# Swapping the halves of a rotary embedding by small DMAs inside SBUF instead of by a matrix product

## The chip, the core and the metric

The kernel runs on one core of one Trainium2 chip. The metric is device time in microseconds (us) for one execution, the median of several; lower is better. Engines: PE is TensorE (matrix products), DVE is VectorE, ACT is ScalarE, POOL is GpSimd, SP is SyncE, which here only issues DMAs, in the order of its program, and waits for semaphores between them.

## The reference

The reference is one hybrid layer followed by two layers of a second kind, over 512 tokens of width 1024. In each layer of the second kind the normalised input is multiplied by a wide weight matrix whose columns are queries, keys and values of several attention mixers, and some of these get a rotary embedding:

```python
def hybrid_mixer(x, w_in, ...):
    h = split_columns(x @ w_in)
    y_a = mla_mixer(h['mla_cq'], h['mla_ckv'], h['mla_krope'], ...)      # rotates krope and 32 of 96 columns of each query head
    y_b = nsa_mixer(h['nsa_q'], h['nsa_k_cmp'], ...)                     # rotates its queries and keys
    y_c = dsa_mixer(h['dsa_q'], h['dsa_k'], ..., h['idx_q'], h['idx_k'], ...)   # rotates all of these
    y_d = stick_breaking_mixer(h['sb_q'], h['sb_k'], h['sb_v'])
    ...
```

The rotation of a head of width n takes its first half a and its second half b to (a cos - b sin, b cos + a sin), with an angle for each token and pair. So it needs, beside the value itself, the value of the other half.

## The kernel before

Activations lie with features on the 128 partitions and 512 tokens along the row. All weights come through one stream of slabs, each 128 x 1024 in float32 (eight 128x128 tiles, 512 KB), loaded by SP into a ring of `RAW = 3` buffers (`load_slabs`, L519 to L531). Most slabs are then split for products in three parts: ACT makes a rounded copy `w_hi` (`high_slabs`, L545), POOL or DVE makes the rest `w_lo` (`low_slabs`, L560); these two have a ring of `SPLIT = 3` buffers. A raw buffer of a split slab is free when its `w_lo` is made; that of a slab used unsplit is free when the last product that reads it is done. ACT takes its part of the splitting in program order: before it moves the result of job j out of PSUM it splits all slabs up to two behind that job's own, and for each it waits until the slab has landed.

The stage that the change touches is `gemm_phase` as `Layer.run` calls it, once for each of the two layers of the second kind. Its jobs are, in order:

- 14 jobs of 24 products (8 tiles, three products each; one slab each): kvcmp, dki, iq0, iq1, cq0, cq1, ckv, kk, nq0, nq1, dq0, dq1, sq0, sq1. Four unsplit slabs, used by short products of the helper `Compress` (L2560), lie in the stream between the slabs of iq1 and cq0, cq0 and cq1, cq1 and ckv, ckv and kk
- 4 jobs mq0 to mq3 (the query heads of the first mixer; two float32 tiles each, all on one unsplit slab)
- 4 jobs uk0 to uk3 and 2 jobs uv0, uv1 on the next unsplit slab, which `Compress` also reads for its last products (L2568, L2570). They are followed in the stream by the slabs of sk0 and sk1, the first that the stage behind uses

Work of other helpers is put between the jobs by `Features`: index scores of one mixer (PE L2694, ACT L2703, DVE L2718 and L2715), sums of squares (ACT L865, PE L836), and splits of finished keys and queries (ACT L2744, L2762, DVE L2749, L2767, POOL L2758). The stage uses three PSUM banks for the jobs in turn: job j's product waits until job j-3's result is moved out (`taken`). At its end all engines meet (L392) before the next stage, an attention, begins.

Thirteen jobs have a rotary embedding: kvcmp, dki, iq0, iq1, kk, nq0, nq1, dq0, dq1, mq0 to mq3. For each, in this order:

1. ACT moves the sum out of PSUM to its tile of `big` (L693) and signals `taken`.
2. PE multiplies that tile by a 128x128 matrix of 0, 1 and -1, in float32, into PSUM bank 4 or 5 (L651). In PE's program this product stands behind the whole next job.
3. DVE multiplies the product by the sine table into a scratch tile (L714), the tile by the cosine table (L716), and adds the two (L718), which signals `joined`.

DVE does step 3 of job j-1 in its step j, ahead of the helpers' work of that step, and so on in program order. SP's part of the stage is the loading of slabs alone.

Of the kernel before, what the change touches and what calls it, by code (L numbers as in the profile page):

```python
# [21 lines left out]
P = 128  # L22
T = 512
QB = T // P
D = 1024
KD = D // P
# [36 lines left out]
SLAB = 8  # L63
# [172 lines left out]
for _n in ("h2", "i4", "mq", "kx"):  # L236
    ROPE.add("cos_" + _n, T)
    ROPE.add("sin_" + _n, T)
for _n in ("h2", "i4", "mq", "kx"):
    ROPE.add("rot_" + _n, P)  # L240

VEC1 = Columns()
for _n, _w in (("norm1_g", 8), ("norm2_g", 8), ("b_mq", 4), ("b_mk", 4), ("b_mo", 4), ("b_fq", 4), ("b_fk", 4),
# [12 lines left out]
def constants():  # L256

    c = np.zeros((P, CONST.n), np.float32)
    rope = np.zeros((P, ROPE.n), np.float32)

    def put(name, a):
        where, to = (ROPE, rope) if name in ROPE.at else (CONST, c)
        at, n = where.at[name]
        to[: a.shape[0], at:at + n] = a

    put("ident", np.eye(P))
    put("ones", np.ones((P, P)))
    put("negident", -np.eye(4))
    put("negroot", -np.eye(4) * np.sqrt(128.0))

    def rotation(spans):

        r = np.zeros((P, P))
        for a, n in spans:
            for i in range(n // 2):
                r[a + n // 2 + i, a + i] = -1
                r[a + i, a + n // 2 + i] = 1
        return r

    def tables(spans):  # L280
        cos, sin = np.ones((P, T)), np.zeros((P, T))
        for a, n in spans:
            inv = np.float32(10000.0) ** (-np.arange(0, n, 2, dtype=np.float32) / np.float32(n))
            ang = (np.arange(T, dtype=np.float32)[None, :] * inv.astype(np.float32)[:, None]).astype(np.float32)
            for half in range(2):
                cos[a + half * n // 2:a + (half + 1) * n // 2] = np.cos(ang.astype(np.float64))
                sin[a + half * n // 2:a + (half + 1) * n // 2] = np.sin(ang.astype(np.float64))
        return cos, sin

    for kind, spans in (("h2", [(0, 64), (64, 64)]), ("i4", [(32 * i, 32) for i in range(4)]),  # L290
                        ("mq", [(64, 32)]), ("kx", [(0, 64), (64, 32), (96, 32)])):
        put("rot_" + kind, rotation(spans))
        cos, sin = tables(spans)
        put("cos_" + kind, cos)
        put("sin_" + kind, sin)
    i = np.arange(P)

    before = np.zeros((P, T - P))
    put("causal", np.concatenate([before, np.where(i[None, :] <= i[:, None], 0, NEG)], 1))
    put("strict", np.where(i[None, :] < i[:, None], 0, NEG))  # L300
    put("tri", (i[:, None] <= i[None, :]).astype(float))
    put("chunk_tri", ((i[:, None] <= i[None, :]) & (i[:, None] // CHUNK == i[None, :] // CHUNK)).astype(float))
    ends = np.arange(NCMP) * CMP_STRIDE + CMP_LEN - 1
    seen = ends[None, None, :] <= (np.arange(QB)[None, :, None] * P + i[:, None, None])
    floor = np.full((P, QB, 1), NEG / 10)
    put("cmp_neg", np.concatenate([np.where(seen, 0, NEG), floor], 2).reshape(P, -1))
    put("goes_on", np.tile((np.arange(T) % CHUNK != 0).astype(float), (P, 1)))
    put("rms_eps", np.full((P, 1), RMS_EPS))
    put("ln_eps", np.full((P, 1), LN_EPS))
    put("one", np.ones((P, 1)))  # L310
    return c, rope
# [16 lines left out]
class Core:  # L328
# [189 lines left out]
            self.last_sum[at // SLAB + slab] = self.sums  # L518
        return [self.sums - jobs + 1 + b for b in range(jobs)]  # L519

    def load_slabs(self, sp):

        last = max(self.last_sum) if self.last_sum else -1
        while self.loaded < min(NSLABS, last + 1 + RAW):
            n = self.loaded
            if n >= RAW and n - RAW in SPLIT_AT:
                sp.wait_ge(self.lo_made, SPLIT_AT[n - RAW] + 1)
            elif n >= RAW:
                sp.wait_ge(self.sums_done, self.last_sum[n - RAW])
            sp.dma_start(self.raw[:, n % RAW, :], self.weights[n]).then_inc(self.slab_loaded[n % RAW], 16)  # L530
            self.loaded += 1  # L531
# [88 lines left out]
def gemm_phase(k, jobs, norm=None, scalar=None, vector=None, banks=None, bank=0, between=None, after=None, lows=True):  # L620
# [7 lines left out]
    for j, job in enumerate(jobs):  # L628
        ends += k.use([tiles_of(job)], by_slab=False)
        if between:  # L630
            between.use(j)
    taken, rotated, joined, part = [k.flag(n) for n in ("taken", "rotated", "joined", "rope_part")]
    ropes = [j for j, job in enumerate(jobs) if job.get("rope")]
    banks = banks or (4 if ropes or norm else 8)

    with k.block() as block:
        @block.sync
        def _(sp):
            k.load_slabs(sp)

        @block.tensor
        def _(pe):
            if norm:
                norm.tensor(pe)

            def rotate(r):
                job = jobs[ropes[r]]
                pe.wait_ge(taken, k.at(taken, ropes[r] + 1))
                if r >= 2:
                    pe.wait_ge(k.flag("rope_part"), k.at(k.flag("rope_part"), 2 * r - 3))  # L650
                nc.tensor.matmul(k.ps[:, 4 + r % 2, :], k.rope("rot_" + job["rope"]), job["out"],  # L651
                                 start=True, stop=True).then_inc(rotated, 1)

            if between:
                between.tensor(pe, -1)
            for j, job in enumerate(jobs):
                if j >= banks:
                    pe.wait_ge(taken, k.at(taken, j - banks + 1))
                for signal in after.get(j, ()) if after else ():
                    pe.wait_ge(*signal)  # L660
                for c, (part, i, cols, start, stop) in enumerate(job["sum"]):
                    if i is not None:
                        k.need(pe, i)
                    if "wait_tile" in job:
                        job["wait_tile"](pe, c)
                    for m, (lhsT, rhs) in enumerate(part):
                        mm = nc.tensor.matmul(k.ps[:, bank + j % banks, cols], lhsT, rhs, start=(start and m == 0),  # L667
                                              stop=(stop and m == len(part) - 1))
                mm.then_inc(k.sums_done, 1)
                if j - 1 in ropes:  # L670
                    rotate(ropes.index(j - 1))
                if between:
                    between.tensor(pe, j)
            if len(jobs) - 1 in ropes:
                rotate(len(ropes) - 1)

        @block.scalar
        def _(act):
# [20 lines left out]
        if ropes or norm or vector or between:  # L699
            @block.vector  # L700
            def _(dve):
# [6 lines left out]
                for j in range(len(jobs) + 1):  # L708
                    if j - 1 in ropes:
                        r, job = ropes.index(j - 1), jobs[j - 1]  # L710
                        rows = slice(0, job.get("rope_rows", P))
                        turned, to = k.scr[rows, 10 + r % 2, :], job["out"][rows]
                        dve.wait_ge(rotated, k.at(rotated, r + 1))
                        nc.vector.tensor_tensor(turned, k.ps[rows, 4 + r % 2, :], k.rope("sin_" + job["rope"])[rows],  # L714
                                                ALU.mult).then_inc(part, 1)
                        nc.vector.tensor_tensor(to, to, k.rope("cos_" + job["rope"])[rows], ALU.mult).then_inc(part, 1)  # L716
                        dve.wait_ge(part, k.at(part, 2 * r + 2))
                        nc.vector.tensor_tensor(to, to, turned, ALU.add).then_inc(joined, 1)  # L718
                    if between and j < len(jobs):
                        between.vector(dve, j)  # L720
# [9 lines left out]
        norm.passed()  # L730
    if between:
        between.passed()
    k.passed(taken=len(jobs), rotated=len(ropes), joined=len(ropes), rope_part=2 * len(ropes))


def token_phase(k, x, jobs, norm, loads=(), bias_here=None, first=0, taken="taken"):
# [2274 lines left out]
def copy_in_phase(k, x, first, later, norm):  # L3011

    nc, s = k.nc, norm.s
    norm.lands = False
    tile_here = [k.flag(f"x_here{c}") for c in range(KD)]
    first_here, here = k.flag("norm_here"), k.flag("inputs_here")
    with k.block() as block:
        @block.sync
# [34 lines left out]
        def _(pe):  # L3053
            pe.wait_ge(first_here, k.at(first_here, 16 * len(first)))
            pe.wait_ge(tile_here[0], 16)
            for _ in range(5):
# [3 lines left out]
            pe.wait_ge(s["squared"], norm.at("squared", KD))  # L3060
            nc.tensor.matmul(k.ps[:, 5, :], k.c("ones"), norm.square_at(KD - 1), start=False, stop=True)\
                .then_inc(s["sq_summed"], 1)
    return here, 16 * len(later)


# [147 lines left out]
def layer_start(k, l, norm):  # L3213
# [3 lines left out]
    ln1 = ResidNorm(k, "ln1_g", "ln1_b")  # L3217
    glu_phase(k, *w["ffn1"], norm, ln1)
    token_phase(k, lambda c: (k.in_hi[:, c, :], k.in_lo[:, c, :]), [(w["v"], lambda tb: big[:, tb, :], None)], ln1,
                loads=[(big[:, 33:42, :].rearrange("p a b -> p (a b)"), k.rope_dram)], first=QB, taken="laid")  # L3220


class Layer:
# [15 lines left out]
    def run(self):  # L3239
# [10 lines left out]
        for key, i in at.items():  # L3250
            scale = 64 ** -0.5 if key in ("nq0", "nq1", "dq0", "dq1", "sq0", "sq1") else 1.0
            jobs.append(feature_job(k, x, w[key], tile(i), rope=rope.get(key), scale=scale,
                                    rope_rows=64 if key == "kvcmp" else P))
        names = list(at)
        for h in range(HEADS):
            jobs.append(feature_job(k, lambda c: tile(6 + c), w["uq"][h], tile(25 + h), depth=2, split=False, rope="mq",
                                    scale=96 ** -0.5))
        for h in range(HEADS):
            jobs.append(feature_job(k, lambda c: tile(8), w["uk"][h], tile(29 + h)[0:64], depth=1, split=False,
                                    view=lambda at: at[0:64]))  # L3260
# [184 lines left out]
```

## Time and profile before

| | |
|---|---|
| median of 3 runs | 3339.65 us (3339.61 to 3339.69) |
| the profiled execution's own time | 3335.59 us |
| its span, first to last instruction | 3333.8 us |
| PE busy | 3231.3 us, 97% of the span |
| DVE, ACT, POOL busy | 1483.1, 1272.9, 383.7 us |
| slab loads | 503, of 512 KB |
| the stage with the rotary embeddings | about 1474 to 1594 us, and 2598 to 2717 us |

PE is busy nearly throughout, so its time is close to the kernel's. The duration that the profile gives a product is longer than the distance at which the next follows, since products are pipelined; distances between starts tell what one costs.

### The profile page before, as it was taken

The page shows a single profiled execution, that of the slowest core. Times are in us where ns is not written, and L with a number is a line of the kernel's source. Part 1 is how long each engine was busy: PE and PEld are TensorE (multiplying, and loading weights), DVE is VectorE, ACT ScalarE, POOL GpSimd, SP SyncE. Part 2 cuts the span into 40 slices and gives each one's busy share as a digit, 9 for nine tenths or more (in the row PEclk, how much of TensorE's full clock was granted, in tenths as well). Part 3 has the DMA queues.
Part 4 walks back from the last instruction along what each step waited for, and adds up shares of the span by engine and source line. Part 5 has one row for each costly group of instructions (what it writes and reads, how often), then busy time and mean ns, then how long its engine had stood idle before and what let it go on. Part 6 is the DMA issues. An engine that isn't in the chain of part 4 may idle for free. (4 is left out here: it accounts for less than half of the span.)

```text
span 3333.8 us, 37221 instructions
## 1 busy us (share of the span) xinstructions
PE 3231.3 (97%) x14860; PEld 2558.4 (77%) x14860; DVE 1483.1 (44%) x2260; ACT 1272.9 (38%) x2190; POOL 383.7 (12%) x277
## 2 busy tenths in 40 slices
PE   9999999999999999999979999999999998899998
PEld 7767778878888888877656888878887766578886
DVE  4154532244243333455875433343334478563333
ACT  3344642333132323235654432242222456542222
POOL 0412434400000000003410000000000233000000
PEclk9999999999999999999989999999999999999999
DMA  4211313323333333332001333323332310123332
GB/s 155 89 45 39 101 58 103 99 82 102 95 95 101 95 98 99 95 98 89 26 1 64 93 97 95 95 88 95 97 94 88 130 45 1 32 83 95 101 92 73
DMA packets 76060, 276.91 MB, mean 83 GB/s; under 512 B 8688, under 2 KB 8944, under 8 KB 75632
## 3 DMA queue, kind: packets, MB, share of 16 engines
q1 hardware_dynamic: 75888, 274.54, 26.7%
q8 instruction: 118, 1.93, 0.2%
q14 instruction: 54, 0.44, 0.0%
HBM read 272.41 MB, written 2.10 MB: 82 GB/s over the span
## 5 line engine op out<-in xcount | busy, mean ns | idle before, releaser
L545 ACT ACTIVATE w_hi<-raw_slabs 128x1024 fp32r<-128x1024 f32 x489 | 516.6, 1057 | 1235.5 <-PE ps L585 1128.8
L560 DVE TENSOR_TENSOR w_lo<-raw_slabs,w_hi 128x1024 fp32r<-128x1024 f32 x372 | 455.1, 1224 | 717.1 <-ACT w_hi L545 717.1
L585 PE MATMUL ps<-in_hi,w_hi 128*128 128x512 f32 x1840 | 719.1, 391 | 5.1 <-DVE in_lo L911 5.1
L585 PE MATMUL ps<-in_lo,w_hi 128*128 128x512 f32 x1840 | 715.9, 389 | 0.0
L585 PE MATMUL ps<-in_hi,w_lo 128*128 128x512 f32 x1840 | 715.8, 389 | 0.0
L585 PE MATMUL ps<-parts,w_hi 128*128 128x512 f32 x2240 | 693.5, 391 | 0.9 <-DVE scratch L1528 0.8
L560 POOL TENSOR_TENSOR w_lo<-raw_slabs,w_hi 128x1024 fp32r<-128x1024 f32 x117 | 288.0, 2463 | 2304.6 <-ACT w_hi L545 2287.6
L585 PEld LDWEIGHTS ps<-parts,w_hi 128*128 128x128 f32 x2240 | 420.4, 188 | 92.7 <-issue 4.3
L585 PE MATMUL ps<-parts,w_lo 128*128 128x512 f32 x1120 | 435.8, 389 | 0.0
L585 PEld LDWEIGHTS ps<-in_hi,w_hi 128*128 128x128 f32 x1840 | 345.4, 188 | 83.2 <-DVE in_lo L911 9.2
L585 PEld LDWEIGHTS ps<-in_hi,w_lo 128*128 128x128 f32 x1840 | 345.4, 188 | 72.1
L585 PEld LDWEIGHTS ps<-in_lo,w_hi 128*128 128x128 f32 x1840 | 345.5, 188 | 71.7 <-issue 1.0
L585 PEld LDWEIGHTS ps<-parts,w_lo 128*128 128x128 f32 x1120 | 210.2, 188 | 43.6
L667 PE MATMUL ps<-in_hi,w_hi 128*128 128x512 f32 x584 | 236.7, 405 | 1.2 <-POOL w_lo L560 1.2
L667 PE MATMUL ps<-in_hi,w_lo 128*128 128x512 f32 x584 | 227.6, 390 | 0.0
L667 PE MATMUL ps<-in_lo,w_hi 128*128 128x512 f32 x584 | 227.6, 390 | 0.0
L1314 DVE SCALAR_TENSOR_TENSOR big<-ps,scratch 128x512 f32<-128x512 f32 x88 | 60.6, 691 | 267.5 <-PE ps L585 248.3
L667 PEld LDWEIGHTS ps<-in_hi,w_hi 128*128 128x128 f32 x584 | 109.7, 188 | 31.6 <-issue 6.5
L667 PEld LDWEIGHTS ps<-in_lo,w_hi 128*128 128x128 f32 x584 | 109.7, 188 | 25.6 <-issue 3.8
L667 PEld LDWEIGHTS ps<-in_hi,w_lo 128*128 128x128 f32 x584 | 109.6, 188 | 23.3
L2063 ACT ACTIVATE scratch<-ps,stats 128x384 f32<-128x384 f32 (+4 forms) x176 | 85.4, 485 | 89.6 <-DVE stats L2034 70.8
L1890 PE MATMUL ps<-const_cols,scratch 128*128 128x128 f32 (+1 forms) x472 | 92.0, 291 | 18.2 <-ACT scratch L1938 15.9
(304 smaller groups left out, 3549.9 us busy)
## 6 DMA issues: line engine op xcount, KB each, us to landing
raw_slabs<-weights SPq DMA_DIRECT2D x503, 512.0 KB, 3.6
big<-rope SPq DMA_DIRECT2D x2, 2304.0 KB, 8.6
x_resid<-xT SPq DMA_DIRECT2D x8, 256.0 KB, 4.6
outT<-x_resid SPq DMA_DIRECT2D x8, 256.0 KB, 2.0
const_cols<-consts SPq DMA_DIRECT2D x1, 836.0 KB, 9.5
scratch<-brow SPq DMA_DIRECT2D x1, 768.0 KB, 10.1
vector_cols<-vec SPq DMA_DIRECT2D x2, 45.5 KB, 9.7
vector_cols<-vec SPq DMA_DIRECT2D x1, 68.5 KB, 3.5
```

The lines of the kernel that those rows point to most:

```text
L545: self.nc.scalar.activation(self.w_hi[:, m % SPLIT, :], self.raw[:, n % RAW, :], ACT.Copy)\
L560: (self.nc.gpsimd if i is None else self.nc.vector).tensor_tensor(self.w_lo[:, m % SPLIT, :], self.raw[:, n % RAW, :], self.w_hi[:, m % SP ...
L585: mm = k.nc.tensor.matmul(out, lhsT, rhs, start=(c == 0 and m == 0), stop=(last and m == 2))
L667: mm = nc.tensor.matmul(k.ps[:, bank + j % banks, cols], lhsT, rhs, start=(start and m == 0), stop=(stop and m == len(part) - 1))
L1314: nc.vector.scalar_tensor_tensor(made(f), k.ps[:, 2 * (f % 3) + 1, :], 0.5, k.scr[:, f % 2, :], ALU.mult, ALU.mult).then_inc(hidden, 1)
L1890: mm = k.nc.tensor.transpose(k.ps[0:w, bank, a:a + P], p[:, a:a + w], k.c("ident"))
L2063: nc.scalar.activation(probs(i)[:, 0:u.width], k.ps[:, bank(i), 0:u.width], ACT.Exp, bias=col(0, i), scale=u.scale, accum_out=col(1, i)).t ...
```

## The change

The rotation matrices are gone (the table that is loaded for each layer shrinks from 9 to 8 tiles of 128x512). In their place SP copies the halves: for each rotated span of n rows one DMA takes its upper n/2 rows of `big` to the lower place of a scratch tile, and one the reverse. That is 2 DMAs for kvcmp and for each of mq0 to mq3, 6 for dki, 8 for iq0 and for iq1, 4 for each of kk, nq0, nq1, dq0 and dq1: 52 in a layer, of 16 or 32 rows of 2 KB each. SP waits for the sum to be moved out (`taken`) and, from the third rotary job on, for the join of the rotary job two before (`joined`), whose scratch tile it fills anew. DVE then multiplies the scratch tile in place by a sine table that carries the sign, and goes on as before.

SP's program therefore alternates: ahead of the copies of each rotary job it issues those slab loads whose buffers can be free by then (up to five slabs past the job's own), and all others behind its copies. The rest of the loads come after the copies of mq3.

```diff
-    def load_slabs(self, sp):
+    def load_slabs(self, sp, upto=NSLABS):
         last = max(self.last_sum) if self.last_sum else -1
-        while self.loaded < min(NSLABS, last + 1 + RAW):
+        while self.loaded < min(NSLABS, last + 1 + RAW, upto + 1):
...
+    moves, landed = [], [0, 0]
+    for r, j in enumerate(ropes):
+        moves.append([(to, to + half, n // 2) for a, n in ROPE_SPANS[jobs[j]["rope"]] if a < jobs[j]["rope_rows"].stop
+                      for to, half in ((a, n // 2), (a + n // 2, -(n // 2)))])
+        landed[r % 2] += 16 * len(moves[r])
+        jobs[j]["swaps"] = landed[r % 2]
...
         @block.sync
         def _(sp):
+            for r, j in enumerate(ropes):
+                slab = max(tiles_of(jobs[j])) // SLAB
+                most = slab + (RAW if slab in SPLIT_AT else RAW - 1)
+                while most < slab + RAW + 2 and (most + 1 - RAW in SPLIT_AT or most + 1 - RAW <= slab - 1):
+                    most += 1
+                k.load_slabs(sp, most)
+                sp.wait_ge(taken, k.at(taken, j + 1))
+                if r >= 2:
+                    sp.wait_ge(joined, k.at(joined, r - 1))
+                for to, src, n in moves[r]:
+                    sp.dma_start(k.scr[to:to + n, 10 + r % 2, :], jobs[j]["out"][src:src + n]).then_inc(swapped[r % 2], 16)
             k.load_slabs(sp)
...
-            def rotate(r):
-                job = jobs[ropes[r]]
-                pe.wait_ge(taken, k.at(taken, ropes[r] + 1))
-                if r >= 2:
-                    pe.wait_ge(k.flag("rope_part"), k.at(k.flag("rope_part"), 2 * r - 3))
-                nc.tensor.matmul(k.ps[:, 4 + r % 2, :], k.rope("rot_" + job["rope"]), job["out"],
-                                 start=True, stop=True).then_inc(rotated, 1)
-
...
-                if j - 1 in ropes:
-                    rotate(ropes.index(j - 1))
...
-                        dve.wait_ge(rotated, k.at(rotated, r + 1))
-                        nc.vector.tensor_tensor(turned, k.ps[rows, 4 + r % 2, :], k.rope("sin_" + job["rope"])[rows],
+                        dve.wait_ge(swapped[r % 2], k.at(swapped[r % 2], job["swaps"]))
+                        nc.vector.tensor_tensor(turned, turned, k.rope("sin_" + job["rope"])[rows],
                                                 ALU.mult).then_inc(part, 1)
```

The mq jobs' cosine, sine and add now act on their 32 rotated rows only, instead of on 128. Semaphores of the first phase are reused for the copies.

## Rows read from the trace of the kernel before

**Rows 1.** The page: busy time of each engine, its share of the span.
```profile
PE 3231.3 (97%) x14860; PEld 2558.4 (77%) x14860; DVE 1483.1 (44%) x2260; ACT 1272.9 (38%) x2190; POOL 383.7 (12%) x277
```

**Rows 2.** Line L651, the rotation product: duration (ns), first and last start.
```profile
L651 PE MATMUL ps<-big x52: 590/591/667, 1484.7 to 2711.3; 128*128 128x512 f32 x52
```

**Rows 3.** Timeline of PE around a rotation product (one row left out): start, us, engine, line.
```profile
1484.49 0.39 PE L667 MATMUL ps<-in_hi,w_lo 128*128 128x512 f32 x1
1484.72 1.02 PE L651 MATMUL ps<-big 128*128 128x512 f32 x2
...
1485.82 0.40 PE L667 MATMUL ps<-in_lo,w_hi 128*128 128x512 f32 x1
```

**Rows 4.** Timeline between iq1's and cq1's products: ACT, PE, SP, POOL.
```profile
1497.61 0.60 ACT L693 ACTIVATE big<-ps 128x512 f32<-128x512 f32 x1 [4.80 <-PE ps L667]
...
1500.17 0.80 SPq L530 DMA_DIRECT2D raw_slabs<-weights  x2
...
1504.97 2.36 POOL L560 TENSOR_TENSOR w_lo<-raw_slabs,w_hi 128x1024 fp32r<-128x1024 f32 x1 [9.29 <-ACT w_hi L545]
...
1508.09 0.48 PE L667 MATMUL ps<-in_hi,w_hi 128*128 128x512 f32 x1
```

**Rows 5.** Timeline of ACT, and one PE row, around dq0 and dq1.
```profile
1551.11 0.60 ACT L693 ACTIVATE big<-ps 128x512 f32<-128x512 f32 x1 [3.16 <-PE ps L667]
...
1557.90 0.58 ACT L693 ACTIVATE big<-ps 128x512 f32<-128x512 f32 x1
...
1559.45 0.44 PE L2694 MATMUL ps<-parts 128*128 128x384 f32 x1 [0.23 <-ACT scratch L2703]
```

**Rows 6.** Timeline of the stage's end, DVE and POOL.
```profile
1574.10 3.32 DVE L2718 SCALAR_TENSOR_TENSOR big<-scratch,big 128x512 f32<-128x512 f32 x4 [1.79 <-ACT scratch L2703]
...
1583.09 0.68 DVE L714 TENSOR_TENSOR scratch<-ps,big 128x512 f32<-128x512 f32 x1
...
1586.44 0.68 DVE L714 TENSOR_TENSOR scratch<-ps,big 128x512 f32<-128x512 f32 x1
...
1591.60 0.69 DVE L718 TENSOR_TENSOR big<-big,scratch 128x512 f32<-128x512 f32 x1
...
1581.35 4.61 POOL L2758 TENSOR_TENSOR parts<-big,parts 64x512 fp32r<-64x512 f32 x3
```

**Rows 7.** Timeline of the stage's end: SP, ACT, PE.
```profile
1583.94 0.33 SPq L530 DMA_DIRECT2D raw_slabs<-weights  x1
...
1587.44 1.06 ACT L545 ACTIVATE w_hi<-raw_slabs 128x1024 fp32r<-128x1024 f32 x1 [2.89 <-DMA raw_slabs<-weights]
1588.40 0.57 ACT L693 ACTIVATE big<-ps 64x512 f32<-64x512 f32 x1
...
1588.19 2.74 PE L667 MATMUL ps<-big,raw_slabs 128*128 128x512 f32 x6
...
1594.42 0.38 PE L1882 MATMUL ps<-big 128*128 128x32 f32 x2 [1.15 <-PEq L392]
```

**Rows 8.** SP's DMAs: a line's issue (ns); from the page, us to landing.
```profile
L3021 SPq DMA_DIRECT2D x_resid<-xT x8: 384/432/433, 0.7 to 5.0; - x8
...
raw_slabs<-weights SPq DMA_DIRECT2D x503, 512.0 KB, 3.6
...
outT<-x_resid SPq DMA_DIRECT2D x8, 256.0 KB, 2.0
```

**Rows 9.** Lines L714 and L718, DVE: duration min/median/max (ns).
```profile
L714 DVE TENSOR_TENSOR scratch<-ps,big x26: 676/692/693, 1485.8 to 2713.9; 128x512 f32<-128x512 f32 x24, 64x512 f32<-64x512 f32 x2
...
L718 DVE TENSOR_TENSOR big<-big,scratch x26: 683/692/2772, 1487.1 to 2715.2; 128x512 f32<-128x512 f32 x24, 64x512 f32<-64x512 f32 x2
```

**Rows 10.** Windows behind the stage's end; the column after POOL's is PE's granted clock.
```profile
1593.30:1597.30 4.00, 2.21 (x13) 1.98 (x14) 2.15 (x10) 1.92 (x11) 2.35 (x1) 0.93 0.47 135
1597.30:1600.70 3.40, 3.40 (x13) 2.58 (x12) 1.94 (x10) 2.61 (x7) 1.07 (x3) 0.58 0.53 154
...
2720.30:2727.10 6.80, 6.71 (x20) 4.67 (x20) 4.52 (x17) 4.03 (x14) 2.77 (x7) 0.54 0.21 77
```

More of the change, by code:

```diff
@@ L238 @@
     ROPE.add("sin_" + _n, T)
-for _n in ("h2", "i4", "mq", "kx"):
-    ROPE.add("rot_" + _n, P)
+ROPE_SPANS = {"h2": ((0, 64), (64, 64)), "i4": tuple((32 * i, 32) for i in range(4)), "mq": ((64, 32),),
+              "kx": ((0, 64), (64, 32), (96, 32))}
 VEC1 = Columns()
@@ L269, in constants @@
     put("negroot", -np.eye(4) * np.sqrt(128.0))
[L271 to L278, printed above, removed]
     def tables(spans):
@@ L286, in tables @@
                 cos[a + half * n // 2:a + (half + 1) * n // 2] = np.cos(ang.astype(np.float64))
-                sin[a + half * n // 2:a + (half + 1) * n // 2] = np.sin(ang.astype(np.float64))
+                sin[a + half * n // 2:a + (half + 1) * n // 2] = (2 * half - 1) * np.sin(ang.astype(np.float64))
         return cos, sin
-    for kind, spans in (("h2", [(0, 64), (64, 64)]), ("i4", [(32 * i, 32) for i in range(4)]),
-                        ("mq", [(64, 32)]), ("kx", [(0, 64), (64, 32), (96, 32)])):
-        put("rot_" + kind, rotation(spans))
+    for kind, spans in ROPE_SPANS.items():
         cos, sin = tables(spans)
@@ L631, in gemm_phase @@
             between.use(j)
-    taken, rotated, joined, part = [k.flag(n) for n in ("taken", "rotated", "joined", "rope_part")]
+    taken, joined, part = [k.flag(n) for n in ("taken", "joined", "rope_part")]
+    swapped = [k.flag(f"tile_here{n}") for n in range(2)]
     ropes = [j for j, job in enumerate(jobs) if job.get("rope")]
+    moves, landed = [], [0, 0]
[4 more added lines that the diff above has]
+        jobs[j]["swaps"] = landed[r % 2]
     banks = banks or (4 if ropes or norm else 8)
@@ L669, in _ @@
                 mm.then_inc(k.sums_done, 1)
-                if j - 1 in ropes:
-                    rotate(ropes.index(j - 1))
                 if between:
                     between.tensor(pe, j)
-            if len(jobs) - 1 in ropes:
-                rotate(len(ropes) - 1)
         @block.scalar
@@ L710, in _ @@
                         r, job = ropes.index(j - 1), jobs[j - 1]
-                        rows = slice(0, job.get("rope_rows", P))
+                        rows = job["rope_rows"]
                         turned, to = k.scr[rows, 10 + r % 2, :], job["out"][rows]
-                        dve.wait_ge(rotated, k.at(rotated, r + 1))
-                        nc.vector.tensor_tensor(turned, k.ps[rows, 4 + r % 2, :], k.rope("sin_" + job["rope"])[rows],
+                        dve.wait_ge(swapped[r % 2], k.at(swapped[r % 2], job["swaps"]))
+                        nc.vector.tensor_tensor(turned, turned, k.rope("sin_" + job["rope"])[rows],
                                                 ALU.mult).then_inc(part, 1)
@@ L732, in gemm_phase @@
         between.passed()
-    k.passed(taken=len(jobs), rotated=len(ropes), joined=len(ropes), rope_part=2 * len(ropes))
+    k.passed(taken=len(jobs), joined=len(ropes), rope_part=2 * len(ropes), tile_here0=landed[0], tile_here1=landed[1])
 def token_phase(k, x, jobs, norm, loads=(), bias_here=None, first=0, taken="taken"):
@@ L3014, in copy_in_phase @@
     norm.lands = False
-    tile_here = [k.flag(f"x_here{c}") for c in range(KD)]
+    tile_here = [k.flag(f"tile_here{c}") for c in range(KD)]
     first_here, here = k.flag("norm_here"), k.flag("inputs_here")
@@ L3062, in _ @@
                 .then_inc(s["sq_summed"], 1)
+    k.passed(**{f"tile_here{c}": 16 for c in range(KD)})
     return here, 16 * len(later)
@@ L3219, in layer_start @@
     token_phase(k, lambda c: (k.in_hi[:, c, :], k.in_lo[:, c, :]), [(w["v"], lambda tb: big[:, tb, :], None)], ln1,
-                loads=[(big[:, 33:42, :].rearrange("p a b -> p (a b)"), k.rope_dram)], first=QB, taken="laid")
+                loads=[(big[:, 33:41, :].rearrange("p a b -> p (a b)"), k.rope_dram)], first=QB, taken="laid")
 class Layer:
@@ L3252, in run @@
             jobs.append(feature_job(k, x, w[key], tile(i), rope=rope.get(key), scale=scale,
-                                    rope_rows=64 if key == "kvcmp" else P))
+                                    rope_rows=slice(0, 64 if key == "kvcmp" else P)))
         names = list(at)
@@ L3256, in run @@
             jobs.append(feature_job(k, lambda c: tile(6 + c), w["uq"][h], tile(25 + h), depth=2, split=False, rope="mq",
-                                    scale=96 ** -0.5))
+                                    rope_rows=slice(64, 96), scale=96 ** -0.5))
         for h in range(HEADS):
```

## The prediction

> **What bounds the kernel now.** I read the page first: PE is busy 97% of the span [rows 1], so what counts is PE's time and what keeps PE waiting; on another engine an operation is free until PE or the meeting at the stage's end waits for it. Then the line of the rotation product, 52 instructions, two for each of 26 products [rows 2]. Then PE's timeline around one [rows 3]: ordinary products start 0.23 us apart (1484.49, 1484.72). The rotation starts at 1484.72, and the next job's second product at 1485.82; one product (0.23) lies between, so the rotation costs 1.10 - 0.23 = 0.87 us. Its two durations of 0.59 overlap and aren't its price. Last I read the timelines where PE could be made to wait once it runs ahead: the slab behind iq1 [rows 4], ACT around dq1 [rows 5], and the stage's end [rows 6, 7]. The second layer repeats the first there.
>
> **Removed.** 26 x 0.87 = 22.6 us of PE time, if PE could start its next work at once each time, and a wait of PE's for L714 of 1.4 us a layer before mq3's rotation. The four rotations of mq0 to mq3 (3.5 of 11.3 us a layer) lie in the tail, costed below; nine lie ahead of it (7.8 us). What remains of the nine, for one layer:
>
> *Four ahead of cq1* (kvcmp, dki, iq0, iq1: 3.5 us). cq1's slab goes into the buffer of the unsplit slab that PE reads right behind iq1's products. Before, its load left at 1500.17, its `w_lo` was made at 1504.97 + 2.36 = 1507.33, and PE came at 1508.09 [rows 4]: 7.16 us from issue to split, and PE 0.76 later. Now this load stands behind iq1's eight copies. ACT had moved iq1 out at 1497.61 + 0.60 = 1498.21; two rotations earlier (the third stands behind iq1's products) that is 1496.5, and dki's join, which the copies also wait for, is long done. From rows of other DMAs an issue takes 0.33 [rows 7] to 0.43 us [rows 8], so eight take 2.6 to 3.5, and the load leaves at 1499.1 to 1500.0. The slab is split 7.16 later, at 1506.3 to 1507.2, while PE would be there at 1508.09 - 3.48 = 1504.6. So 0.9 to 1.8 us are kept of 3.5; I take 1.3.
>
> *kk and nq0* (1.7): what follows kk's rotation are sums of squares that ACT makes at the same time, so some of it is waited away; I keep 1.3 (0.9 to 1.7).
>
> *nq1 and dq0* (1.7): the last index product behind dq1 waits for ACT (L2694 at 1559.45, idle before it, released by L2703), and ACT comes late to dq1 (1557.90), in one chain of its own work since 1551.11 [rows 5]. From dq0's end (about 1551) on ACT sets the pace; I keep 0.8 (0.4 to 1.7).
>
> *dq1* (0.9): the same shape, ACT's move and its first L2703 before the last index product; I keep 0.4 (0 to 0.9).
>
> Sum ahead of the tail: 1.3 + 1.3 + 0.8 + 0.4 = 3.8 us a layer, between 2.2 and 6.1.
>
> **The tail.** Here I count in the clock of before and subtract the 3.8 at the end. DVE does the index sums behind sq1 from 1574.10 without a break until 1583.09, then the four mq ropes until 1591.60 + 0.69 = 1592.29 [rows 6]. This chain hangs on sq1's products, not on the mq rotations; removing these doesn't shorten it. Step by step:
>
> 1. DVE's first multiply reads PSUM now and will read SBUF with both inputs, as L718 does. L714 never took more than 693 ns, L718 up to 2772 [rows 9]; the long ones lie beside POOL's work. In mq0's rope POOL runs L2758 until 1585.96 [rows 6], and the rope takes 3.35 us (1583.09 to 1586.44) where the other three take 5.85 / 3 = 1.95. With all three operations behind POOL I add one 0.65: mq0 joined at 1587.1, mq1 at 1589.0.
> 2. SP may copy mq3's halves only when mq1 is joined, 1589.0. Two issues and the semaphore: 1589.8 (to 1590.0).
> 3. Only then does SP issue the load of sk1's slab, which before left at 1583.94, as soon as mq3's products had used up its buffer [rows 7]. It lands 3.6 us later [rows 8], at 1593.4.
> 4. ACT is in program order. It waited for this slab before: L545 at 1587.44 was idle 2.89 us for the DMA, and uk0 was moved out only behind it, at 1588.40 [rows 7]. Now L545 starts at 1593.45, and uk0 is out at 1593.45 + 0.96 + 0.6 = 1595.0.
> 5. uk3 needs uk0's bank. Before, uk1, uk2, uk3 started from 1588.19 (six instructions, 0.86 a pair [rows 7]), so uk3 at 1589.9, and the next stage's first product at 1594.42, 4.5 later. Now uk3 starts at 1595.0 and the next stage at 1599.5: **+5.1 us** (4.5 to 5.6). DVE's last rope, with mq3's copies landing between 2.0 us [rows 8] and twice the slab's 3.6 after 1589.8, is done by 1599.0, so a slow copy stays just hidden.
>
> In this tail mq3's products end two rotations sooner, at 1583.9 - 1.7 = 1582.2, and uk0 to uk2 take 2.6 more; PE then has nothing from 1584.8 until 1595.0, some 10 us. Before, a stretch in which PE was busy 2.21 of 4.00 us was followed by 3.4 us at half clock in the first layer, and a like one by 6.8 us in the second (granted clock 0.58 and 0.54 in my windows, which cut the edges) [rows 10], so 1.2 GHz instead of 2.4. After 10 idle us I expect the same for the products from uk3 on. 3.4 to 6.8 us at half clock cost 1.7 to 3.4 us: **+2.5**.
> "TensorE: Matmul & The Clock Gate", section "HAM oscillation — how this bites in real kernels", of the Trainium skill says that PE idling over a DMA wait brings the clock down to half and that the work behind it starts cold. By that rule the 2.5 stands; without it the sum below would be 5.0 us less.
>
> On step 1 the Trainium skill, "SBUF — State Buffer", section "Who interferes with whom", says that a DVE instruction with two SBUF inputs contends with a GpSimd one that reads SBUF, while one with a single SBUF input doesn't. The trace agrees (693 against 2772 ns). Without it step 1 would be 0.65 less, the whole 1.3.
>
> Moved and added elsewhere: other copies are issued while SP would wait for a `w_lo` or a landing anyway, and the ropes of kvcmp to dq1 get their input after 2 to 4 us instead of after a whole job of 5.5, so DVE isn't later; if a copy took 8 us they would be. The smaller table load (8 tiles for 9) is hidden. L716 and L718 stay as they are.
>
> **Sum.** For a layer 5.1 + 2.5 - 3.8 = +3.8 us, for both +7.6. The profiled execution took 3335.59, so 3343.2; the median of the runs, 3339.65, lies 4.06 above that execution, so **3347 us**. Own range: each layer from 4.5 + 1.7 - 6.1 = +0.1 to 5.6 + 3.4 - 2.2 = +6.8, so 3340 to 3353, and up to 3356 if the next stage also runs longer at half clock.
>
> **Rivals.**
> - *PE's clock costs nothing net* (0.29). Half-clock stretches come already right behind the stage's end [rows 10]; if the one in the tail only takes their place, 2.5 drops out: 2 x (5.1 - 3.8) = +2.6, 3342. With most of the nine rotations kept (6.1) it is 3338. Within 0.2%.
> - *The slab isn't late* (0.13), the other side. All hangs on step 3: if DVE joined mq1 before about 1584, SP's load would leave as before, the tail would cost nothing, and the layers gain 3.8 each: 3332; with all 11.3 + 1.4 kept, 3314. For it: the earlier ropes get their input sooner and DVE has idle time ahead of 1574.10 (1.79 us). Against: DVE's work from there to mq0's rope waits for sq1's products, not for ropes.
> - *Copies land slowly* (0.08). If 16-row copies take 8 us or more, the helpers behind each rope on DVE wait, and the last rope ends past 1599: some 2 us a layer at the end and as much before, 3356.
>
> **Chances.** A measurement of this kernel tells about 0.2%, 6.7 us, from no change. Forecast 0.50, the rivals 0.29, 0.13 and 0.08. Faster: 0.12, of the second rival. Same: the first's 0.29, 0.01 of the second and 0.03 of the forecast, 0.33. Slower: 0.47 and 0.08, 0.55. Range 3334 to 3356: it reaches into both rivals and leaves out the second's most and the third's upper part.
>
> **What would show it.** No L651; jobs of 24 products following each other without 0.87 between. PE idle before cq1, 0.8 to 2.5 us, released by POOL's w_lo. SP's load of sk1's slab behind the last two copies; ACT's L545 for it idle 8 us or more for a DMA; PE idle about 10 us in one piece between uk2 and uk3; granted clock near 0.5 behind it; the next stage's first product at about 1598 in the first layer, instead of 1594.42. The prediction is wrong if ACT doesn't wait there, if DVE joins mq1 early, or if the copies' issue on SP costs far from 0.33 to 0.43.

## The result, and the profile after

The changed kernel took 3352.17 us (median of 6 runs, 3344.86 to 3354.33) against 3339.63 for the kernel before on the same chips (6 runs, 3334.65 to 3340.83): a ratio of 1.0039, 95% interval 1.0026 to 1.0052 (here and below the ratio isn't the quotient of the two medians, and can differ from it by 0.1%). It is 0.4% slower, clear of the 0.2% named above, within the range on record (3334 to 3356) and 5 us above the predicted 3347. The profiled execution took 3350.75, its span is 3348.9.

The page of the kernel after, part 1 and two lines of part 6 (answering to [rows 1, 8]):

```profile
PE 3220.6 (96%) x14808; PEld 2556.9 (76%) x14808; DVE 1488.7 (44%) x2260; ACT 1271.2 (38%) x2190; POOL 385.4 (12%) x277
...
scratch<-big SPq DMA_DIRECT2D x48, 64.0 KB, 3.4
...
scratch<-big SPq DMA_DIRECT2D x56, 32.0 KB, 1.9
```

PE is less busy than before and the kernel is longer: the 52 rotation instructions are gone, their time went into waiting. The 104 copies land in 1.9 to 3.4 us in the median. What an issue costs SP stands in the answer for the copies' line (ns, min/median/max):

```profile
L646 SPq DMA_DIRECT2D scratch<-big x104: 507/589/1016, 1484.0 to 2722.0; - x104
```

That is 0.59 us, not the 0.33 to 0.43 of other DMAs. The first place where it is felt is the slab of cq1. Timeline of the kernel after, SP, ACT, POOL, PE (as [rows 4]; the stage began at 1477.72 in this execution, at 1473.84 before):

```profile
1499.68 0.60 ACT L688 ACTIVATE big<-ps 128x512 f32<-128x512 f32 x1 [3.90 <-PE ps L666]
...
1505.28 1.05 SPq L520 DMA_DIRECT2D raw_slabs<-weights  x2
...
1509.07 1.06 ACT L535 ACTIVATE w_hi<-raw_slabs 128x1024 fp32r<-128x1024 f32 x1 [6.83 <-DMA raw_slabs<-weights]
...
1510.20 2.34 POOL L550 TENSOR_TENSOR w_lo<-raw_slabs,w_hi 128x1024 fp32r<-128x1024 f32 x1 [11.45 <-ACT w_hi L535]
...
1512.69 0.77 PE L666 MATMUL ps<-in_hi,w_hi 128*128 128x512 f32 x1 [4.05 <-POOL w_lo L550]
```

iq1 is moved out at 1500.28, eight copies occupy SP until the load can leave at 1505.28, ACT sits idle 6.83 us for the landing, PE 4.05 us for POOL's half. From the stage's start PE reaches cq1's products after 34.97 us; before it was 1508.09 - 1473.84 = 34.25. All four rotations' worth, 3.5 us, is gone and 0.7 more. These products then ran partly at half clock. In the windows below (us, busy times of PE, PEld, DVE, ACT, POOL, then PE's granted clock, where 1.00 is 2.4 GHz and 0.50 is 1.2 GHz) the first is that stretch, with cq1's 24 products in 7.2 us where 5.5 are usual; the second is PE's idle piece in the tail, the third what follows it:

```profile
1512.70:1519.90 7.20, 7.20 (x25) 5.78 (x26) 0.26 (x1) 0.63 (x1) 2.37 (x1) 0.76 0.26 75
1588.00:1599.50 11.50, 0.64 (x2) 0.00 (x0) 8.80 (x12) 1.52 (x3) 1.69 (x2) 0.64 0.19 57
1599.50:1605.50 6.00, 5.94 (x22) 4.59 (x22) 0.00 (x0) 2.57 (x6) 0.00 (x0) 0.55 0.00 0
```

The tail, in the timeline of the kernel after (as [rows 6, 7]):

```profile
1587.07 1.64 DVE L709 TENSOR_TENSOR scratch<-scratch,big 32x512 f32<-32x512 f32 x1
1588.64 1.74 DVE L711 TENSOR_TENSOR big<-big 32x512 f32<-32x512 f32 x1
1590.41 0.68 DVE L713 TENSOR_TENSOR big<-big,scratch 32x512 f32<-32x512 f32 x1
...
1593.74 0.68 DVE L709 TENSOR_TENSOR scratch<-scratch,big 32x512 f32<-32x512 f32 x1 [0.72 <-DMA scratch<-big]
...
1596.98 0.68 DVE L713 TENSOR_TENSOR big<-big,scratch 32x512 f32<-32x512 f32 x1
...
1591.17 3.06 SPq L646 DMA_DIRECT2D scratch<-big  x4
1594.27 0.58 SPq L520 DMA_DIRECT2D raw_slabs<-weights  x1
...
1597.97 1.06 ACT L535 ACTIVATE w_hi<-raw_slabs 128x1024 fp32r<-128x1024 f32 x1 [11.28 <-DMA raw_slabs<-weights]
1598.94 1.53 ACT L688 ACTIVATE big<-ps 64x512 f32<-64x512 f32 x3
...
1599.56 1.22 PE L666 MATMUL ps<-big,raw_slabs 128*128 128x512 f32 x1 [10.93 <-ACT big L688]
...
1606.77 0.38 PE L1877 MATMUL ps<-big 128*128 128x32 f32 x2 [1.16 <-PEq L382]
```

Read it from below. PE idles 10.93 us for ACT, ACT 11.28 us for a DMA, and this DMA left SP at 1594.27, right behind the last four copies; those waited for mq0's and mq1's joins. uk3's product starts 21.2 us after mq0's (1578.33) where it took 15.45, and the next stage follows 7.2 us later where it took 4.5, at a granted clock of 0.55 in the third window. The stage is 129.05 us long (1477.72 to 1606.77) against 120.58 before (1473.84 to 1594.42); in the second layer 129.06 against 120.59. The second layer comes to the same length in another way: more of cq1's products ran at half clock, so mq0 starts 0.9 us later than before, and from uk3 to the next stage it takes 6.2 us, not 7.2.

### The profile page after: what moved, and what is told of

It is laid out like the page before. It is cut to its first block and busy times, and to the rows that moved or that the text cites. A ratio compares the mean times of both kernels' runs of the same rounds, so it can differ in the third digit from the quotient of the medians.

```text
span 3348.9 us, 37221 instructions
## 1 busy us (share of the span) xinstructions
PE 3220.6 (96%) x14808; PEld 2556.9 (76%) x14808; DVE 1488.7 (44%) x2260; ACT 1271.2 (38%) x2190; POOL 385.4 (12%) x277
```

## The experiments

Each kernel is the changed one with the edit shown. Where "the kernel before" is the measure, its runs lie between those of the kernel tried, on the same chips.

**One load moved: the slab of sk1 ahead of mq2's copies.** It waits for mq3's products on PE, and these wait for no copy.

```diff
                     most += 1
+                if jobs[j]["rope"] == "mq" and r == len(ropes) - 2:
+                    most = slab + RAW
                 k.load_slabs(sp, most)
```

> The changed kernel, with one load moved in SP's program: the slab of sk1 is loaded ahead of mq2's copies (it waits for mq3's products, which don't wait for copies) instead of behind mq3's. Queue theory (in-order SP and ACT make the tail's 5.8 us and its half clock 2.7 us a layer): about 8 us a layer less than the changed kernel, 3336 us, ratio to before 0.997 to 1.001, PE's 10.9 us idle piece gone, half-clock stretch behind it gone. Rival (the join chain on DVE, slowed by POOL because the sine product now has two SBUF inputs, sets the tail): at most 1 to 2 us a layer less, about 3350.

Measured: 3335.07 us, before 3333.0; ratio 1.0002 (0.9991 to 1.0013). The tail's loss is gone. Its timeline, SP, ACT, PE and DVE:

```profile
1582.68 0.34 SPq L520 DMA_DIRECT2D raw_slabs<-weights  x1
...
1586.00 1.06 ACT L535 ACTIVATE w_hi<-raw_slabs 128x1024 fp32r<-128x1024 f32 x1 [2.72 <-DMA raw_slabs<-weights]
...
1593.58 0.68 DVE L715 TENSOR_TENSOR big<-big,scratch 32x512 f32<-32x512 f32 x1
...
1587.59 1.12 PE L668 MATMUL ps<-big,raw_slabs 128*128 128x512 f32 x2 [2.37 <-ACT big L690]
...
1594.59 0.61 PE L1879 MATMUL ps<-big 128*128 128x32 f32 x2 [3.53 <-PEq L382]
```

The load leaves at 1582.68, ahead of mq1's join (1589.6), ACT's wait is 2.72 us as it was before the change (2.89 [rows 7]), and PE's idle piece is 2.4 us. DVE's last add ends at 1594.26 and the next stage starts at 1594.59: what sets the tail now is DVE's chain of ropes. From mq0's start to the next stage it is 19.7 us, against 28.4 in the changed kernel and 20.0 before, and the stages are 121.2 and 121.3 us long, 7.8 less than in the changed kernel, as expected. Half clock isn't gone, though: from uk3 to the next stage the granted clock is 0.87 in the first layer and 0.74 in the second, but DVE ends last there. The rival would have left 3350.

**The other load moved: cq1's slab ahead of iq1's eight copies.**

```diff
                     most += 1
+                if jobs[j]["rope"] == "i4" and slab + 1 not in SPLIT_AT:
+                    most = slab + RAW + 1
                 k.load_slabs(sp, most)
```

> The changed kernel, with one other load moved: cq1's slab is loaded ahead of iq1's eight copies instead of behind them. Queue theory: PE's idle 4.05 us ahead of cq1 falls under 0.5, and cq1's products run at full clock (5.5 instead of 7.2 us), so 5 to 6 us a layer less than the changed kernel if the gain isn't waited away later, about 3341 (ratio 1.000 to 1.002). Rival (later in the stage ACT and DVE set the pace, so what is saved ahead of cq1 is waited away behind it): 2 us a layer or less, about 3348.

Measured: 3348.62 us, ratio 1.0041 (1.0025 to 1.0056). SP and PE in its first layer:

```profile
1500.84 0.33 SPq L520 DMA_DIRECT2D raw_slabs<-weights  x1
1501.28 4.93 SPq L648 DMA_DIRECT2D scratch<-big  x8
...
1508.04 0.47 PE L668 MATMUL ps<-in_hi,w_hi 128*128 128x512 f32 x1
```

PE doesn't wait before cq1 there (0.66 us in the second layer) and cq1's first product comes 30.9 us after the stage's start, so the wait was the load's place in the queue. The stages are 123.3 and 127.0 us long in this profile, 5.7 and 2.0 less than in the changed kernel, while the tail keeps its 11 us idle piece. The first layer is what the queue theory said, the second what the rival said. The two layers run the same program; of the 3.7 us between them 1.6 arise from ckv to kk, where a stretch at half clock lies in the second layer alone, and 1.3 from uk3 on, where the granted clock is 0.75 in the first and 0.59 in the second. In the whole, 3348.62 and 1.0041 are the rival's total, and the interval leaves the queue theory's 1.000 to 1.002 out; what became of the rest of the 8 us in the traced stages is taken up under *The sum*.

**Both loads moved.**

> Both moves in one kernel. Queue theory: the two add up, some 13.5 us a layer less than the changed kernel, 3325 us, ratio to before 0.995 to 0.997, faster than both. Rival (the copies themselves, 52 a layer at 0.6 us of SP each and 2 to 4 us to land, cost DVE's helpers their time): no better than before, ratio 0.999 to 1.001.

Measured: 3325.72 us, before 3333.0; ratio 0.9979 (0.9967 to 0.9991). This is faster than the kernel before by 0.2%, and by 0.6% than the changed one. Against the kernel with sk1's slab alone moved (1.0002) the second move is worth 0.23%, where by itself it was worth nothing that could be told. The stages are 118.1 and 115.5 us, against 120.6 before: 10.9 and 13.5 less than in the changed kernel, where some 13.5 had been expected in both, and the ratio misses the 0.995 to 0.997 narrowly. It lies below the rival's 0.999 to 1.001, which the interval's upper end, 0.9991, just touches.

**No exchange at all.** Neither product nor copy: DVE multiplies the tile itself by the sine table, so the exchange of halves is left out.

```diff
-            for r, j in enumerate(ropes):
...
-                    sp.dma_start(k.scr[to:to + n, 10 + r % 2, :], jobs[j]["out"][src:src + n]).then_inc(swapped[r % 2], 16)
             k.load_slabs(sp)
...
-                        dve.wait_ge(swapped[r % 2], k.at(swapped[r % 2], job["swaps"]))
-                        nc.vector.tensor_tensor(turned, turned, k.rope("sin_" + job["rope"])[rows],
+                        dve.wait_ge(taken, k.at(taken, j))
+                        for signal in after.get(j, ()) if after else ():
+                            dve.wait_ge(*signal)
+                        nc.vector.tensor_tensor(turned, to, k.rope("sin_" + job["rope"])[rows],
```

> The changed kernel without any exchange of halves: no copies, no waits for them, SP loads slabs as before; DVE multiplies the tile itself by the sine table (it leaves out the exchange). It bounds what the removal of 26 rotation products can be worth. Queue theory: ahead of the tail some 6 us a layer are gained, in the tail DVE's chain stays, 0 to 1 us: 3325 to 3328, ratio 0.996, and the kernel with both loads moved comes within 3 us of it. Rival (PE time is worth its full price): 22.6 + 2.8 us, 3314, ratio 0.9925. Rival of contention (the sine product with two SBUF inputs is what costs): 3335 or more.

Measured: 3323.79 us, ratio 0.9970 (0.9959 to 0.9982). So taking the 26 products away, with nothing in their place, is worth 0.30%, some 10 us, and not 22.6. The stages are 114.4 and 114.3 us, 6.2 less than before, as expected, where 12.7 a layer were removed. mq0 starts 5.1 us sooner in the first layer, so of the 7.8 ahead of the tail 2.7 are waited away, for POOL's `w_lo` ahead of ckv (0.8) and for ACT; of the 4.9 in the tail 1.1 remain. There DVE's ropes end last in the first layer (0.33 us ahead of the next stage), ACT's last moves behind PE at half clock in the second (0.31 us ahead). The kernel with both loads moved is 2 us from this bound, so copies that stand in the right order cost little. The rivals' 3314 and 3335 are both excluded.

**The changed kernel again**, as the comparison for the next three.

> The changed kernel itself once more, as the comparison for the other three of this call. Every theory: 1.003 to 1.005 of before, each of the two stages 8.5 us longer than before.

Measured: 3350.57 us, before 3333.46; ratio 1.0047 (1.0035 to 1.0059). The stages are 128.7 and 131.0 us long, 8.1 and 10.4 more than before; the 10.4 wasn't expected, and again the second layer's cq1 products and its end ran longer at half clock.

**PE kept busy in the idle piece.**

```diff
                 if between:
                     between.tensor(pe, j)
+                if ropes and j == ropes[-1] + 3:
+                    k.keep_busy(pe, 46, bank=4)
```

> The changed kernel with 46 products of 0.23 us on constants, into an unused PSUM bank, put behind uk2, into PE's 10.9 us idle piece. Clock theory: the products from uk3 on run at 2.4 GHz, 2.7 us a layer less from there to the next stage (4.5 instead of 7.2), 5.4 us or 0.16% less than the changed kernel; the wait itself stays, so still slower than before, 1.002. Rival (the clock falls anyway, or the half clock there costs nothing since ACT's moves set the pace): the same 7.2 us, 1.004.

Measured: 3346.75 us, ratio 1.0048 (1.0033 to 1.0063). Its timeline of PE:

```profile
1587.66 11.03 PE L396 MATMUL ps<-masks 128*128 128x512 f32 x46
1599.21 1.13 PE L666 MATMUL ps<-big,raw_slabs 128*128 128x512 f32 x2 [0.51 <-ACT big L690]
...
1603.83 0.38 PE L1879 MATMUL ps<-big 128*128 128x32 f32 x2 [1.16 <-PEq L382]
```

and a window over uk3 and what follows (columns as above):

```profile
1599.20:1602.40 3.20, 3.19 (x21) 2.56 (x21) 0.00 (x0) 2.35 (x5) 0.00 (x0) 1.00 0.00 0
```

The clock is full, and from uk3 to the next stage it takes 4.6 us in both layers, instead of 7.2 and 7.3 in the first layer of the changed kernel's two traces and 6.2 and 7.4 in the second. So the half clock behind the idle piece cost 2.6 us in the first layer and 1.6 to 2.8 in the second. The stages are 126.2 and 127.7 us long instead of 128.7 and 131.0; in the second 0.6 of the difference lies ahead of mq0, where the edit changes nothing. In the whole the medians differ by 3.8 us and the ratios not at all: the whole doesn't confirm it.

**Two copies instead of eight for iq0 and for iq1**, the same bytes; the wrong rows are exchanged there.

```diff
+        if jobs[j]["rope"] == "i4":
+            moves[r] = [(0, 64, 64), (64, 0, 64)]
         landed[r % 2] += 16 * len(moves[r])
```

> The changed kernel with two copies instead of eight for each of iq0 and iq1, of 64 rows each (it exchanges the wrong rows there). Issue-cost theory (0.6 us of SP for each copy, as the changed kernel's trace shows, is what makes cq1's slab late): cq1's slab leaves 6 x 0.6 = 3.6 us sooner and PE's 4.05 us idle ahead of cq1 shrinks to about 0.5, its products run at full clock. Rival (the copies' data on the DMA engines delays the slab; the bytes are the same here): the idle stays near 4. In the total, as with the load moved ahead for cq1 alone, 1.002 to 1.004, since ACT and the tail give part of it back.

Measured: 3339.58 us, ratio 1.0024 (1.0014 to 1.0034). cq1's first product in the first layer:

```profile
1514.52 0.47 PE L668 MATMUL ps<-in_hi,w_hi 128*128 128x512 f32 x1 [0.20 <-POOL w_lo L550]
```

It waited 0.20 us where the changed kernel waits 4.05, and comes 31.1 us after the stage's start (1483.41) instead of 35.0. In the second layer it waited 0.32. The stages are 123.2 and 123.8 us long. A copy of 64 rows occupied SP 0.51 or 0.60 us, as one of 16 rows does. With bytes equal and issues fewer, the number of issues is what made the slab late.

**Both loads moved, and scratch tiles of their own for mq2 and mq3.** Their copies no longer wait for mq0's and mq1's joins; they have semaphores of their own too.

```diff
+    places = [10 + r % 2 for r in range(len(ropes) - 2)] + [8, 9]
+    lane = [r % 2 for r in range(len(ropes) - 2)] + [2, 3]
...
-                    sp.wait_ge(joined, k.at(joined, r - 1))
+                    sp.wait_ge(joined, k.at(joined, min(r - 1, len(ropes) - 4)))
...
-                    sp.dma_start(k.scr[to:to + n, 10 + r % 2, :], jobs[j]["out"][src:src + n]).then_inc(swapped[r % 2], 16)
+                    sp.dma_start(k.scr[to:to + n, places[r], :], jobs[j]["out"][src:src + n]).then_inc(swapped[lane[r]], 16)
```

> Both loads moved, and mq2's and mq3's copies go to scratch tiles of their own, so they don't wait for mq0's and mq1's join. If the join chain through SP still sets the tail: the next stage begins 1.0 to 1.5 us sooner a layer than with both loads moved, ratio 0.997, and the changed kernel's four mq ropes on DVE follow each other without a wait for a DMA. If DVE's own work sets it (each rope 1.95 us, the first 4 us beside POOL): 0.5 to 0.7 us a layer, the DVE idle that is seen between mq1's and mq2's rope, and no change that can be told.

Measured: 3324.60 us, ratio 0.9976 (0.9965 to 0.9987), not to be told from 0.9979. On DVE mq1's last and mq2's first operation now follow each other; in the kernel with both loads moved there were 0.70 us between, for the copy:

```profile
1586.49 0.68 DVE L719 TENSOR_TENSOR big<-big,scratch 32x512 f32<-32x512 f32 x1
1587.09 0.68 DVE L715 TENSOR_TENSOR scratch<-scratch,big 32x512 f32<-32x512 f32 x1
...
1590.33 0.68 DVE L719 TENSOR_TENSOR big<-big,scratch 32x512 f32<-32x512 f32 x1
...
1591.21 0.32 ACT L2587 ACTIVATE big<-ps 31x64 f32<-31x64 f32 x2
...
1591.83 0.38 PE L1883 MATMUL ps<-big 128*128 128x32 f32 x2 [1.15 <-PEq L382]
```

The 0.7 us on DVE are gone, but from mq0's start to the next stage it is 19.35 and 19.28 us, only 0.3 and 0.6 less than with both loads moved (19.64 and 19.89). The first reading's 1.0 to 1.5 is excluded. The second reading is near, but DVE no longer ends last: its last add ends at 1591.01, ACT's last move, behind products at a granted clock of 0.73, at 1591.53, and the next stage starts 0.3 us behind that. So DVE's ropes and ACT's moves are within 0.5 us of each other at the stage's end, and taking the wait away gains only until the second of them. The total can't tell it.

## Why the prediction came out as it did

The direction and the mechanism of the tail were right; one term ahead of it had the wrong size and sign, and one wasn't in the sum. The total came nearer than the working did: at +8.5 us a layer both stages lie outside the range that was worked out for a layer (+0.1 to +6.8), and with their +16.9 the total would be 3356.5. It falls into the prediction's own 3340 to 3353 because the whole grew by 12.5 only: in the traces 4.6 us came back between the stages, which nothing in the prediction foresaw (see *The sum*). That is luck. For the first layer, from the stage's start:

| term, us | predicted | measured |
|---|---|---|
| kept of the four rotations ahead of cq1 | 1.3 | -0.7 |
| half clock on cq1's products | 0 | +1.7 longer |
| kept from there to mq0's start (kk, nq0, nq1, dq0, dq1) | 2.5 | 2.4 |
| mq0's to uk3's start | +5.1 | +5.8 |
| uk3's start to the next stage | +2.5 | +2.7 |
| the layer | +3.8 | +8.5 |

The third row is cq1's end, 1519.89 - 1477.72 = 42.17 us after the start against 39.80 before, and mq0's start, 100.61 against 100.62. So at mq0 nothing is left of nine rotations.

*The step that failed* is "from rows of other DMAs an issue takes 0.33 to 0.43 us, so eight take 2.6 to 3.5". A copy inside SBUF took 0.59, and with the gaps iq1's eight took SP from 1500.3 to 1505.3. From the load to the split it was 7.26 us (1505.28 to 1512.54), as estimated (7.16). Everything else in the step held: the 2 us of extra issue time are the 2 us between +1.3 and -0.7. The kernel with two copies for eight and the one with the load moved both take the wait away, by two routes. The prediction had named an issue cost far from 0.33 to 0.43 as a sign of being wrong.

*Not foreseen* was the clock there: it was at half level behind this wait as well, 1.7 us in this execution, more in the second layer. It goes with the first error: in both layers of the four traces where PE waited 3.9 to 4.5 us for cq1, its products ran at a granted clock of 0.64 to 0.77; where the wait was under 1 us they ran at 1.00, but for one layer of the last kernel (0.77 behind 0.83 us). At the predicted wait of 1.7 to 2.6 us the question wasn't asked.

*ACT as pace-maker behind cq1* was sized right, in its parts too: 1.1, 0.8 and 0.5 us were kept where 1.3, 0.8 and 0.4 were written. The kernel without any exchange shows the same thing as a whole: 6.2 us a stage is all that the removal is worth. *L716 and L718 stay as they are* holds for what they do, not for how long they take: before, one such operation in each layer ahead of the tail took 2.8 us and one 1.7 beside POOL's work; now the ropes run at other times, and in the first layer four take 2.8 to 2.9. PE doesn't wait for DVE ahead of the tail in that layer, so no cost of it shows.

*The tail*, steps 1 to 5: the sine product now runs into POOL's work, and mq0's rope took 3.95 us (1587.07 to 1591.02) where it was 3.35, 0.60 for the 0.65 written. mq3's copies, the load, ACT's wait, uk3 behind uk0 came in that order; the load left 15.9 us after mq0's start, 0.6 later than estimated, again by the issues and the semaphores. Moving this one load removed 8.7 us of the tail in the first layer (28.4 to 19.7) and 7.9 in the second (27.5 to 19.6), so the order of SP's queue and ACT's program is its cause, not DVE. The clock's 2.5 is 2.6 in the first layer, and 1.6 to 2.8 in the second, by the experiment that keeps PE busy. The rival *PE's clock costs nothing net* is refuted in the traced stages, and between them nothing is given back (997.9 us there, 998.5 in the changed kernel); the totals don't tell. The Trainium skill's rule ("TensorE: Matmul & The Clock Gate", "HAM oscillation — how this bites in real kernels") agreed with granted clocks of 0.55 behind 10.93 idle us and 1.00 when there was work in them; so did that of "SBUF — State Buffer", "Who interferes with whom", with the 0.60: beside POOL's L2753 the sine product took 1.64 us, where with one input in PSUM it had taken 0.68 beside the same work.

*The slab isn't late* failed where it was said to: mq1 was joined at 1593.0, not before the load could leave. *Copies land slowly* failed: 1.9 to 4.1 us.

*The sum.* Two stages give +16.9 us, the medians +12.5, the profiled executions +15.2. The difference of the spans, 15.1, is 3.9 ahead of the first stage, 8.5, -4.6 between the stages, 8.5 and -1.1 behind. Outside the stages the two programs are the same but for the smaller table load, and most of the difference is the granted clock. Ahead of the first stage the changed kernel's execution had 10.2 us at half clock and the other none. Between the stages 3.9 of the 4.6 arise in one part of 170 PE instructions. Here it is in the kernel before, the changed one, and the one with cq1's slab alone moved (columns as above):

```profile
1701.00:1739.10 38.10, 31.69 (x173) 20.27 (x173) 26.16 (x46) 19.77 (x51) 0.00 (x0) 0.89 0.00 0
1712.70:1746.90 34.20, 27.78 (x173) 17.68 (x173) 26.72 (x47) 19.91 (x52) 0.00 (x0) 1.00 0.00 0
1705.90:1743.30 37.40, 30.97 (x172) 19.84 (x172) 26.69 (x47) 20.07 (x52) 0.00 (x0) 0.91 0.00 0
```

This part took 34.2 us in each of the seven traces with full clock in it, 35.9, 37.4 and 38.1 us in the three with 3.4, 6.8 and 8.4 us at half clock. So moving cq1's slab alone gained 7.7 us in the traced stages and lost 3.2 here and 1.3 behind the second stage; its profiled execution took 3346.45 us against 3350.75. A gain of 4 us is lost between six runs of 3346.1 to 3352.7 and the changed kernel's 3344.9 to 3354.3. Two copies for eight, with full clock in this part, gave 0.23% (1.0047 to 1.0024). What stays open is what decides where the half clock falls: from one trace each it can't be told whether the edit of SP's order moves it or chance does.

## What to carry to other kernels

An operation that is moved from a saturated engine to a queue is paid for by what stands behind it in that queue: before a copy with a wait is put on the engine that issues the loads, write down which load is next and who stops in program order until it has landed. Here the reordering of two loads turned 0.4% slower into 0.2% faster, and with nothing at all in its place the removed work gave 0.3%, since half of it (6.2 of 12.7 us a layer) was waited away for other engines. Count DMAs by their issue time, measured for the same kind of transfer, before counting their bytes.

## What the runs showed of the hardware

A DMA of 16 or 32 rows of 2 KB from SBUF to SBUF occupied SP 0.59 us in the median, one of 128 rows of 4 KB from HBM 0.328. The smaller transfer has the longer issue. Part of it is the company: iq1's first copy took 0.51 and the seven right behind it 0.59 each, and the two loads right behind those took 0.58 and 0.43.

The add of a rope took DVE 0.68 us on 32 rows (L713) and 0.69 on 128 (L718 before), away from POOL's work, so leaving out three quarters of the rows in the mq jobs was worth nothing.

The half clock comes and goes in parts whose code is the same. In an execution of the kernel with both loads moved, a window in the first block, where PE is busy throughout and where its longest idle time in the 50 us before was 0.43 us, read:

```profile
254.00:272.00 18.00, 18.00 (x54) 11.08 (x54) 4.74 (x18) 4.75 (x18) 0.00 (x0) 0.53 0.00 1
```

and in the profiled execution of the kernel before:

```profile
254.00:272.00 18.00, 18.00 (x96) 11.48 (x96) 7.88 (x28) 8.32 (x31) 0.00 (x0) 1.00 0.00 0
```

54 products against 96 in the same 18 us; the same 70 products in and around it took 21.7 us in the first and 13.7 in the second. The same stretch at half clock stands in the traces of the kernel without any exchange and of the one with two copies for eight. The first execution took 3334.36 us, where seven others of the same kernel took 3323.2 to 3326.5 and four 3330.6 to 3336.0. One such stretch is worth as much as a stage's whole change, which is why stage lengths from the traces carry the argument here and the totals only confirm what is over some 5 us.
